# Prompt attention: a head's weighted sum over its last 512 queries issued as one piece of eight key blocks, behind the next head's second row block

## The chip, the cores and the metric

The kernel runs on one core of a Trainium2 chip. The metric is the device time of one execution in microseconds (us). Three runs of the kernel before gave 2279.73, 2285.48 and 2282.09 us, so the median is 2282.09 us.

## What is computed

The program is one inference step of a small decoder trunk with 1024 prompt tokens (and 32 sample tokens). After the first layer and the shared keys and values come 16 heads of causal attention of the prompt with itself, with a learned decay. Cut to what matters here:

```
s = einsum('bqhd,bkhd->bhqk', q, k) * (1.0 / sqrt(HEAD_DIM))      # HEAD_DIM = 64
decay = cq[..., :, None] - ck[..., None, :]                       # cumulative log forget sums
s = where(k_pos[None, :] <= q_pos[:, None], s + decay, -inf)
p = softmax(s, axis=-1)
o = einsum('bhqk,bkhd->bqhd', p, v)                               # the weighted sum
```

After it come the output projection and the second layer's MLP.

## The kernel before, in words

A head's 1024 queries are cut into 8 row blocks of 128. A row block has a running number `n` over all heads, 0 to 127; `n % 8` is its place `i` in the head, and it has `(i + 1) * 128` keys. Four engines pass a row block on, each in a loop over `n` that is written out in a fixed order:

- TensorE (PE), `prompt_pe`: `score(n + 3)` multiplies queries and keys for the row block three ahead (L1635, L1636, and the causal mask last, L1639). `turn(n)` transposes the probabilities of row block `n`, 128 keys at a time (L1650), into two PSUM banks that take turns, four transposes to a bank.
- VectorE (DVE), `prompt_dve`: in turn `n` it does `norm(n + 1)` (a reciprocal, L1744, and a scaling of the row block, L1747), sometimes `out` (two copies of a finished weighted sum out of PSUM, L1755), and `top(n + 3)` (the row maximum of the scores, L1739).
- ScalarE (ACT), `prompt_act`: in turn `n` it copies the transposes of row block `n` out of PSUM into `pT` (`turned(n)`, L1723) and then does the exponentials of row block `n + 3` (`exp(n + 3)`, L1712).
- GpSimd (POOL) splits the finished sums of two heads into a high and a low part (L1786 and L1788), once in two heads for each half of the queries.

The weighted sum of a head is done in two halves of 512 queries. `weigh(n, kb0, kb1)` adds the key blocks `kb0` to `kb1 - 1` of the half that row block `n` ends, with matmuls that fill 64 columns of the array each, two side by side (L1674 and L1678, behind the diagonal L1676 and L1680). The first half has four key blocks and stands at `n % 8 == 4`. The second half has eight. Before the change it stands in two pieces behind the next head's row blocks: key blocks 0 to 3 after `turn` of the next head's first row block (`n % 8 == 0`), key blocks 4 to 7 after `turn` of its third (`n % 8 == 2`). The piece with key block 0 waits until ACT has copied all transposes of the head (`t_ev`), and until the bank's last sum has been copied out (`o_ev`). DVE copies the second half out in its turn `n % 8 == 3`, and the first half of the head before in its turn `n % 8 == 1`.

Between these, in turns 14 to 17, PE does the last weighted sums of the sample tokens (`weigh_sample`, L1418, and `turn_sample`, L1440), which DVE copies out in `spread_sample` (L1557).

The loads of the next heads' queries, keys and values are issued by the SP queue, which waits for `q_full` and `o_full`.

Of the kernel before, what the change touches and what calls it, by code (L numbers as in the profile page):

```python
# [26 lines left out]
def decoder_step(nc, ins, outs):  # L27
# [18 lines left out]
    NQ = T // P  # L46
# [15 lines left out]
    with ExitStack() as ctx:  # L62
# [1368 lines left out]
        def weigh_sample(pe, u, bank):  # L1431
            pe.wait_ge(s_vg[u], 64)
            pe.wait_ge(p_ev, 2 * (u + 1))
            pe.wait_ge(s_in, 16)
            weigh_part(pe, u, bank, (0, 1, 2)).then_inc(s_pv, 1)

        def turn_sample(pe, u, bank):
            pe.wait_ge(s_osb, u + 1)
            for q in range(4):
                last = pe.transpose(ps[:, bank, q * P:(q + 1) * P], o_sb[:, q * P:(q + 1) * P], ident[:, :])  # L1440
            last.then_inc(s_otr, 1)
# [140 lines left out]
        def probs_of(i, c0, c1):  # L1582
            if P_AT[i] == 4:
                return p_hi2[:, c0:c1]
            return p_lo4[:, P_AT[i] * 512 + c0:P_AT[i] * 512 + c1]

        def quads_to(n):
            return 12 * (n // NQ) + sum(i // 4 + 1 for i in range(n % NQ))
# [29 lines left out]
        def prompt_pe(pe):  # L1618
            pe.wait_ge(one_rows, 2)

            def score(n):
                hh, i = divmod(n, NQ)
                e, w = hh % 2, (i + 1) * P
                if i == 0:
                    pe.wait_ge(stacked[e], STACK * (hh // 2 + 1))
                if n >= S_BACK[i]:
                    pe.wait_ge(q_exp, n - S_BACK[i] + 1)
                if n == 0:
                    pe.wait_ge(v_ev, 2 * NTT)
                if n == 3:  # L1630
                    pe.wait_ge(s_oc, 4 * 2)
                b = S_AT[i]
                for s in range(0, w, 512):
                    c = min(512, w - s)
                    pe.matmul(ps[:, b + s // 512, 0:c], q_a[e][:, i * P:w], k_a[e][:, s:s + c], start=True, stop=False)  # L1635
                    pe.matmul(ps[:, b + s // 512, 0:c], q_b[e][0:HD + 2, i * P:w], k_b[e][0:HD + 2, s:s + c],  # L1636
                              start=False, stop=(s + c < w))
                at_ = i * P % 512
                pe.matmul(ps[:, b + i * P // 512, at_:at_ + P], ident_b[:, :], causal_b[:, :], start=False,  # L1639
                          stop=True).then_inc(q_full, 1)  # L1640

            def turn(n):
                i = n % NQ
                pe.wait_ge(q_nrm, n + 1)
                for s in range(0, i + 1, 4):
                    nq = quads_to(n) + s // 4
                    if nq >= 2:
                        pe.wait_ge(t_ev, nq - 1)
                    for kb in range(s, min(s + 4, i + 1)):
                        last = pe.transpose(ps[:, 4 + nq % 2, (kb - s) * P:(kb - s + 1) * P],  # L1650
                                            probs_of(i, kb * P, (kb + 1) * P), ident[:, :])
                    last.then_inc(t_full, 1)

            def weigh(n, kb0, kb1):


                hh, g = n // NQ, n // 4 % 2
                av = 2 * hh + g
                if kb0 == 0:
                    pe.wait_ge(t_ev, quads_to(n + 1))  # L1660
                    pe.wait_ge(v_in[hh % 2], 16 * (hh // 2 + 1))
                    if av >= 2:
                        pe.wait_ge(o_ev, 2 * (av - 1))
                    if av == 0:
                        pe.wait_ge(s_oc, 4)
                    if av == 1:
                        pe.wait_ge(p_ev, 8)
                    if av == 4:
                        pe.wait_ge(s_oc, 4 * 4)
                for kb in range(kb0, kb1):  # L1670
                    x = pT[g][:, kb, :].rearrange("p (r c) -> p r c", c=P)
                    d, v, bank = kb - 4 * g, v_h[hh % 2][:, kb, :], 6 + av % 2
                    if d <= 0:
                        pe.matmul(ps[0:HD, bank, 0:2 * P], v, x[:, 0:4:3, :], start=(kb == 0), stop=False)  # L1674
                    else:
                        outer = pe.matmul(ps[0:HD, bank, P:2 * P], v, x[:, 3, :], start=False, stop=(d == 3))  # L1676
                    if d <= 1:
                        pe.matmul(ps[HD:P, bank, 0:2 * P], v, x[:, 1:3, :], start=(kb == 0), stop=False)  # L1678
                    elif d == 2:
                        pe.matmul(ps[HD:P, bank, P:2 * P], v, x[:, 2, :], start=False, stop=True).then_inc(o_full, 1)  # L1680
                    else:
                        outer.then_inc(o_full, 1)

            for n in range(3):
                score(n)
            for n in range(NBLK):
                if n + 3 < NBLK:
                    score(n + 3)
                turn(n)
                if n % NQ == 4:  # L1690
                    weigh(n - 1, 0, 4)
                elif n % NQ in (0, 2) and n >= NQ:
                    weigh(n - n % NQ - 1, 2 * (n % NQ), 2 * (n % NQ) + 4)
                if n == 14:
                    pe.wait_ge(o_ev, 6)
                    weigh_sample(pe, 2, O_BANK[2])
                if n == 15:
                    turn_sample(pe, 2, O_BANK[2])
                if n == 16:
                    pe.wait_ge(s_oc, 4 * 3)  # L1700
                    weigh_sample(pe, 3, O_BANK[3])
                if n == 17:
                    turn_sample(pe, 3, O_BANK[3])
            weigh(NBLK - 1, 0, NQ)
# [442 lines left out]
        @block.tensor  # L2147
        def _(pe):

            front_pe(pe)  # L2150
            mlps[0].pe(pe)
            heads_pe(pe)
            sample_pe_end(pe)
            pe.wait_ge(const_ready, 13)
            prompt_pe(pe)
            proj_o.pe(pe)
            mlps[1].pe(pe)
# [64 lines left out]
```

## Time and profile before

| | |
|---|---|
| median of three runs | 2282.09 us |
| the profiled execution, its own time | 2281.51 us |
| its span, first to last instruction | 2278.5 us |
| PE busy | 2236.0 us (98%) |
| DVE, ACT, POOL busy | 1036.8, 575.6, 612.8 us |
| stretch of the prompt attention | 1176 to 1436 us |
| in it PE, DVE, ACT busy | 242.05, 205.92, 182.12 us |
| one head in the steady part | 15.1 us (two heads 30.15) |

A PE busy of 98% is made by the MLPs ahead of the attention and behind it. In the attention the engines wait for one another in turn, so that stretch is read from its own rows: who waits for whom, and what stands in time order around the place that the change moves. "Idle before" in brackets is how long the engine did nothing before that row and what ended it.

### The profile page before, as it was taken

The page shows a single profiled execution, that of the slowest core. Times are in us where ns is not written, and L with a number is a line of the kernel's source. Part 1 is how long each engine was busy: PE and PEld are TensorE (multiplying, and loading weights), DVE is VectorE, ACT ScalarE, POOL GpSimd, SP SyncE. Part 2 cuts the span into 40 slices and gives each one's busy share as a digit, 9 for nine tenths or more (in the row PEclk, how much of TensorE's full clock was granted, in tenths as well). Part 3 has the DMA queues.
Part 4 walks back from the last instruction along what each step waited for, and adds up shares of the span by engine and source line. Part 5 has one row for each costly group of instructions (what it writes and reads, how often), then busy time and mean ns, then how long its engine had stood idle before and what let it go on. Part 6 is the DMA issues. An engine that isn't in the chain of part 4 may idle for free.

```text
span 2278.5 us, 36833 instructions
## 1 busy us (share of the span) xinstructions
PE 2236.0 (98%) x14447; PEld 2077.3 (91%) x14447; DVE 1036.8 (46%) x1760; ACT 575.6 (25%) x1264; POOL 612.8 (27%) x445
## 2 busy tenths in 40 slices
PE   8999999999999999999999999999999999999999
PEld 8999999999999977777776777999999999999999
DVE  7842332433333676543146888335333433324332
ACT  5420110110101333333145777322110100101101
POOL 6233333333333522100001112353333333322240
PEclk9999999999999999999999999999999999999999
DMA  5111111111111114445565654011111111111112
GB/s 154 41 47 47 47 47 47 46 47 43 43 47 47 66 65 150 153 130 165 179 171 119 144 117 107 28 47 47 47 47 44 45 43 47 47 47 47 47 56 77
DMA packets 195852, 170.01 MB, mean 75 GB/s; under 512 B 28880, under 2 KB 169472, under 8 KB 195687
## 3 DMA queue, kind: packets, MB, share of 16 engines
q1 hardware_dynamic: 155493, 141.50, 21.8%
q10 hardware_dynamic: 40202, 26.23, 3.7%
q8 instruction: 122, 2.00, 0.4%
q14 instruction: 35, 0.29, 0.0%
HBM read 137.55 MB, written 30.50 MB: 74 GB/s over the span
## 4 chain that ended last, share of the span: by engine, by line
PE 86%; DVE 7%; ACT 3%; DMA 2%; issue 1%; POOL 0%; SPq 0%; ACTq 0%; DVEq 0%
PE ps L368 35%; PE ps L633 29%; PE ps L881 12%; DVE stat L1739 2%; PE ps L495 2%; ACT pT L1723 1%; PE ps L1674 1%; DMA k_b<-cum_dram 1%; DVE p_lo L1747 1%; PE ps L896 1%; PE ps L1922 1%; PE ps L1650 1%; PE ps L1376 1%; PE ps L1396 1%; DVE tmp_b L445 1%
## 5 line engine op out<-in xcount | busy, mean ns | idle before, releaser
L368 PE MATMUL ps<-xn_hi,w_lo 128*128 128x352 f32 x1528 | 494.9, 324 | 4.9 <-DVE h L711 4.2
L368 PE MATMUL ps<-xn_lo,w_hi 128*128 128x352 f32 x1528 | 489.8, 321 | 0.0
L368 PE MATMUL ps<-xn_hi,w_hi 128*128 128x352 f32 x1528 | 489.4, 320 | 0.0
L633 PE MATMUL ps<-hid_hi,w_lo 128*128 128x352 f32 x1440 | 464.5, 323 | 0.0
L633 PE MATMUL ps<-hid_lo,w_hi 128*128 128x352 f32 x1440 | 461.9, 321 | 0.0
L633 PE MATMUL ps<-hid_hi,w_hi 128*128 128x352 f32 x1440 | 461.4, 320 | 0.0
L335 POOL CAST w_hi<-w_raw 128x1024 fp32r<-128x1024 f32 x132 | 139.2, 1055 | 994.9 <-issue 506.2
L711 DVE TENSOR_TENSOR h<-ps,h 128x352 f32<-128x352 f32 x360 | 185.8, 522 | 413.1 <-PE ps L633 413.1
L672 ACT ACTIVATE tmp_b<-tmp_a 128x352 f32<-128x352 f32 x192 | 94.9, 498 | 1076.6 <-DVE tmp_a L694 1076.6
L337 POOL TENSOR_TENSOR w_lo<-w_raw,w_hi 128x1024 fp32r<-128x1024 f32 x132 | 319.1, 2417 | 10.6
L368 PEld LDWEIGHTS ps<-xn_hi,w_lo 128*128 128x128 f32 x1528 | 286.6, 188 | 7.9 <-DVE h L711 5.3
L368 PEld LDWEIGHTS ps<-xn_lo,w_hi 128*128 128x128 f32 x1528 | 287.1, 188 | 0.5
L368 PEld LDWEIGHTS ps<-xn_hi,w_hi 128*128 128x128 f32 x1528 | 286.4, 187 | 0.0
L633 PEld LDWEIGHTS ps<-hid_lo,w_hi 128*128 128x128 f32 x1440 | 270.5, 188 | 0.0
L633 PEld LDWEIGHTS ps<-hid_hi,w_lo 128*128 128x128 f32 x1440 | 270.2, 188 | 0.0
L633 PEld LDWEIGHTS ps<-hid_hi,w_hi 128*128 128x128 f32 x1440 | 269.9, 187 | 0.0
L694 DVE SCALAR_TENSOR_TENSOR tmp_a<-ps,rms 128x352 f32<-128x352 f32 x192 | 99.3, 520 | 372.7 <-PE ps L368 372.4
L698 DVE TENSOR_TENSOR hid_lo<-tmp_b,hid_hi 128x352 fp32r<-128x352 f32 x192 | 224.3, 1219 | 60.9 <-ACT hid_hi L675 60.9
L881 PE MATMUL ps<-kv_lo,xn_hi 128*128 128x512 f32 (+1 forms) x400 | 162.1, 405 | 1.5 <-issue 0.8
L881 PE MATMUL ps<-kv_hi,xn_hi 128*128 128x512 f32 (+1 forms) x400 | 157.5, 394 | 0.0
L881 PE MATMUL ps<-kv_hi,xn_lo 128*128 128x512 f32 (+1 forms) x400 | 157.2, 393 | 0.0
L1739 DVE TENSOR_REDUCE stat<-ps 128x1 f32<-128x128 f32 (+7 forms) x128 | 96.3, 752 | 35.5 <-PE ps L1639 35.0
(266 smaller groups left out, 2828.3 us busy)
## 6 DMA issues: line engine op xcount, KB each, us to landing
w_raw<-in_w_up SPq DMA_DIRECT2D x64, 512.0 KB, 4.0
w_raw<-in_w_down SPq DMA_DIRECT2D x60, 512.0 KB, 3.4
out<-tok_out ACTq DMA_DIRECT2D x32, 256.0 KB, 2.2
qk_dram<-turn_hi ACTq DMA_DIRECT2D x32, 256.0 KB, 2.4
qk_dram<-turn_lo ACTq DMA_DIRECT2D x32, 256.0 KB, 2.9
k_page<-in_cache_k SPq DMA_DIRECT2D x32, 256.0 KB, 3.4
v_page<-in_cache_v SPq DMA_DIRECT2D x16, 512.0 KB, 9.5
q_a<-qk_dram SPq DMA_DIRECT2D x32, 256.0 KB
```

Of the source, the lines that this page charges most:

```text
L335: pool.tensor_copy(hi[:, par, :], w_raw[:, par, :]).then_inc(w_split, 1)
L337: pool.tensor_tensor(lo[:, par, :], w_raw[:, par, :], hi[:, par, :].bitcast(F32), ALU.subtract).then_inc(w_split, 1)
L368: last = pe.matmul(ps[:, bank, 0:CH], w, x(k, c), start=(k == 0 and i == 0), stop=(k == nk - 1 and i == 2))
L445: eng.tensor_tensor(tmp_b[:, c, :], tmp_b[:, c, :], self.slots[self.sum_at(m, c) % len(self.slots)], ALU.add).then_inc(self.acc, 1)
L495: last = pe.matmul(ps[:, n % 2, 0:CH], w, x, start=(k == 0 and i == 0), stop=(k == GT - 1 and i == 2))
L633: last = pe.matmul(ps[:, NC * (dm % 2) + c, 0:CH], w, x, start=(k == 0 and i == 0), stop=(k == GT - 1 and i == 2))
L672: act.activation(tmp_b[:, c, :], tmp_a[:, c, :], ACT.Square).then_inc(self.sq, 1)
L694: dve.scalar_tensor_tensor(tmp_a[:, c, :], ps[:, NC * (j % 2) + c, 0:CH], 0.0, rms[:, c], ALU.max, ALU.mult).then_inc(self.relu, 1)
L698: dve.tensor_tensor(hid_lo[:, self.uhalf * GT + j, chunk(c)], tmp_b[:, c, :], hid_hi[:, self.uhalf * GT + j, chunk(c)].bitcast(F32), ALU.s ...
L711: dve.tensor_tensor(h[:, dm, chunk(c)], ps[:, NC * (dm % 2) + c, 0:CH], h[:, dm, chunk(c)], ALU.add).then_inc(self.added, 1)
L881: last = pe.matmul(ps[0:w, g % 4, :], x, y, start=(k == 0 and j == 0), stop=(k == KT - 1 and j == 2))
L1739: dve.tensor_reduce(stat[:, 0, n % 4:n % 4 + 1], scores_of(i), AX, ALU.max, negate=True).then_inc(q_max, 1)
```

## The change

In PE's loop, the second half's weighted sum is no longer issued in two pieces of four key blocks at `n % 8 == 0` and `n % 8 == 2`. It is issued in one piece of eight at `n % 8 == 1`, behind the scores of the next head's fifth row block (640 keys) and the transposes of its second. Nothing else is edited; no instruction is added or taken away, and the rows of DVE, ACT, POOL and SP keep their order.

```
                 turn(n)
                 if n % NQ == 4:
                     weigh(n - 1, 0, 4)
-                elif n % NQ in (0, 2) and n >= NQ:
-                    weigh(n - n % NQ - 1, 2 * (n % NQ), 2 * (n % NQ) + 4)
+                elif n % NQ == 1 and n >= NQ:
+                    weigh(n - 2, 0, NQ)
                 if n == 14:
```

The order on PE, at a head's end in the middle of the loop, between the transpose of the next head's first row block and its second. `k_a` and `q_a` are keys and queries, `p_lo` the probabilities, `pT` their transposes, `v_h` the values. Before, the last two matmuls of the first piece and what follows them:

```order
L1674 MATMUL ps<-pT_154,v_h_158 64x256
L1678 MATMUL ps<-pT_154,v_h_158 64x256
L1635 MATMUL ps<-k_a_148,q_a_144 128x512
L1636 MATMUL ps<-k_b_150,q_b_146 128x512
L1635 MATMUL ps<-k_a_148,q_a_144 128x128
L1636 MATMUL ps<-k_b_150,q_b_146 128x128
L1639 MATMUL ps<-causal_b,ident_b 128x128
L1650 MATMUL ps<-ident,p_lo_151 128x128 x2
```

After the change, from the transpose of the first row block on:

```order
L1650 MATMUL ps<-ident,p_lo_151 128x128
L1635 MATMUL ps<-k_a_148,q_a_144 128x512
L1636 MATMUL ps<-k_b_150,q_b_146 128x512
L1635 MATMUL ps<-k_a_148,q_a_144 128x128
L1636 MATMUL ps<-k_b_150,q_b_146 128x128
L1639 MATMUL ps<-causal_b,ident_b 128x128
L1650 MATMUL ps<-ident,p_lo_151 128x128 x2
L1674 MATMUL ps<-pT_154,v_h_158 64x256
```

The scores over 640 keys no longer have a piece of the weighted sum ahead of them.

The order on PE at the next step, ahead of the scores over 768 keys (sixth row block). Before, they come straight behind the two transposes:

```order
L1650 MATMUL ps<-ident,p_lo_151 128x128 x2
L1635 MATMUL ps<-k_a_148,q_a_144 128x512
L1636 MATMUL ps<-k_b_150,q_b_146 128x512
L1635 MATMUL ps<-k_a_148,q_a_144 128x256
L1636 MATMUL ps<-k_b_150,q_b_146 128x256
L1639 MATMUL ps<-causal_b,ident_b 128x128
```

After the change, the end of the piece of eight and what follows it:

```order
L1676 MATMUL ps<-pT_154,v_h_158 64x128
L1678 MATMUL ps<-pT_154,v_h_158 64x256
L1676 MATMUL ps<-pT_154,v_h_158 64x128
L1680 MATMUL ps<-pT_154,v_h_158 64x128
L1676 MATMUL ps<-pT_154,v_h_158 64x128
L1635 MATMUL ps<-k_a_148,q_a_144 128x512
L1636 MATMUL ps<-k_b_150,q_b_146 128x512
L1635 MATMUL ps<-k_a_148,q_a_144 128x256
L1636 MATMUL ps<-k_b_150,q_b_146 128x256
L1639 MATMUL ps<-causal_b,ident_b 128x128
```

All 15 matmuls of the second half now stand between those transposes and the 768-key scores.

The order on PE in turns 17 and 18, where the sample's last transposes (`o_sb`) stand. Before:

```order
L1650 MATMUL ps<-ident,p_lo_151 128x128 x2
L1440 MATMUL ps<-ident,o_sb 128x128 x4
L1635 MATMUL ps<-k_a_147,q_a_143 128x512
L1636 MATMUL ps<-k_b_149,q_b_145 128x512
L1635 MATMUL ps<-k_a_147,q_a_143 128x256
```

After the change:

```order
L1676 MATMUL ps<-pT_154,v_h_159 64x128
L1680 MATMUL ps<-pT_154,v_h_159 64x128
L1676 MATMUL ps<-pT_154,v_h_159 64x128
L1440 MATMUL ps<-ident,o_sb 128x128 x4
L1635 MATMUL ps<-k_a_147,q_a_143 128x512
```

The sample's transposes too now have the whole piece ahead of them.

## Rows read from the trace of the kernel before

**Rows 1.** Busy time by stretch: the attention, then two heads of it.

```profile
core 0: us, PE busy (x) PEld busy (x) DVE busy (x) ACT busy (x) POOL busy (x), PEclk, DMA share, GB/s
...
1176.00:1436.00 260.00, 242.05 (x1993) 180.89 (x1994) 205.92 (x456) 182.12 (x450) 37.38 (x36) 0.98 0.56 131
...
1316.72:1346.88 30.16, 28.58 (x227) 21.54 (x226) 25.33 (x56) 22.38 (x56) 3.77 (x4) 1.00 0.55 123
```

**Rows 2.** Waits of DVE in twelve steady heads (total us, times, longest).

```profile
DVE stat L1739 <- PE ps L1639: 18.5, 36, 0.8
```

**Rows 3.** Chain of waits through a head's end (start us, us, what).

```profile
1324.70 0.60 ACT pT L1723
...
1328.25 0.82 DVE stat L1739
```

**Rows 4.** PE in time order, same head's end (start us, us, engine, line, operation).

```profile
1324.98 0.28 PE L1650 MATMUL ps<-ident,p_lo 128*128 128x128 f32 x1
1325.35 0.43 PE L1674 MATMUL ps<-pT,v_h 128*64 128x256 f32 x1
...
1326.91 0.38 PE L1674 MATMUL ps<-pT,v_h 128*64 128x256 f32 x1
...
1327.22 0.50 PE L1635 MATMUL ps<-k_a,q_a 128*128 128x512 f32 x1
...
1327.98 0.23 PE L1639 MATMUL ps<-causal_b,ident_b 128*128 128x128 bf16 x1
1328.05 0.39 PE L1650 MATMUL ps<-ident,p_lo 128*128 128x128 f32 x2
...
1328.99 0.23 PE L1639 MATMUL ps<-causal_b,ident_b 128*128 128x128 bf16 x1
...
1329.48 0.43 PE L1674 MATMUL ps<-pT,v_h 128*64 128x256 f32 x1
...
1330.72 0.50 PE L1635 MATMUL ps<-k_a,q_a 128*128 128x512 f32 x1
```

**Rows 5.** DVE in time order, same head's end.

```profile
1326.54 0.87 DVE L1755 COPY oT<-ps 64x256 f32<-64x256 f32 x2
1328.25 0.82 DVE L1739 TENSOR_REDUCE stat<-ps 128x1 f32<-128x640 f32 x1 [0.84 <-PE ps L1639]
...
1329.59 0.95 DVE L1739 TENSOR_REDUCE stat<-ps 128x1 f32<-128x768 f32 x1
```

**Rows 6.** PE, the head's end before that one.

```profile
1309.87 0.43 PE L1674 MATMUL ps<-pT,v_h 128*64 128x256 f32 x1
```

**Rows 7.** DVE, the head's end before that one.

```profile
1311.06 0.88 DVE L1755 COPY oT<-ps 64x256 f32<-64x256 f32 x2
...
1314.18 0.94 DVE L1739 TENSOR_REDUCE stat<-ps 128x1 f32<-128x768 f32 x1
```

**Rows 8.** POOL, the head's end before that one.

```profile
1312.69 1.28 POOL L1788 TENSOR_TENSOR o_lo<-oT,o_hi 128x512 fp32r<-128x512 f32 x1
```

**Rows 9.** PE's weight loads at the edges of the two pieces.

```profile
1318.34 0.13 PEld L1674 LDWEIGHTS ps<-pT,v_h 128*64 128x64 f32 x1 [0.17 <-issue]
...
1327.22 0.19 PEld L1635 LDWEIGHTS ps<-k_a,q_a 128*128 128x128 f32 x1 [0.39 <-issue]
```

**Rows 10.** PE at the sample's last transposes.

```profile
1221.63 0.60 PE L1440 MATMUL ps<-ident,o_sb 128*128 128x128 f32 x4
```

**Rows 11.** DVE at the copies behind them.

```profile
1222.35 0.60 DVE L1557 COPY o_s<-ps 64x32 f32<-64x32 f32 x4
```

**Rows 12.** PE where the third head's scores begin.

```profile
1203.58 0.48 PE L1635 MATMUL ps<-k_a,q_a 128*128 128x128 f32 x1 [2.59 <-DMA k_b<-cum_dram]
```

**Rows 13.** PE, three places with a longer wait or behind one.

```profile
1322.14 0.95 PE L1650 MATMUL ps<-ident,p_lo 128*128 128x128 f32 x7 [1.08 <-ACT pT L1723]
...
1413.45 0.98 PE L1650 MATMUL ps<-ident,p_lo 128*128 128x128 f32 x7 [1.93 <-DVE p_lo L1747]
...
1414.90 1.97 PE L1650 MATMUL ps<-ident,p_hi 128*128 128x128 f32 x8
```

**Rows 14.** Busy time and granted clock (PEclk) behind the longest of those waits.

```profile
1414.00:1416.00 2.00, 1.96 (x13) 1.67 (x11) 1.96 (x4) 1.64 (x6) 1.92 (x2) 0.71 0.78 234
```

## Prediction, made before the changed kernel was run

> **What bounds the kernel now.** I read the page first: PE is busy 98% of the span, but that is the MLPs. The busy time by stretch [rows 1] singles out the attention: in its 260.0 us PE is busy 242.05, DVE 205.92, ACT 182.12, so no engine fills it. Two steady heads take 30.16 us, of which PE works 28.58 and DVE 25.33. The waits [rows 2] say who is late: in twelve heads DVE's row maximum waits 36 times, 18.5 us in all, for PE's causal mask, the last matmul of a score block. The chain of waits [rows 3] shows when: ACT copies the last transposes out until 1325.30, PE then starts the first piece of the weighted sum, and DVE's next row on the chain is the 640-key maximum at 1328.25. From there the chain stays on DVE until the exponentials of the head's last row block, then passes to ACT and PE, and so to the next head's end. So one head costs what this ring costs, and the place the change moves lies on it.
>
> **The parts, for one head's end.** Nothing is added or removed: 15 weighted-sum matmuls move on PE. What counts is when DVE gets the 640-key and the 768-key scores.
>
> What goes. The first piece no longer stands ahead of the 640-key scores. DVE had finished the copies at 1326.54 + 0.87 = 1327.41 and waited 0.84 us for them [rows 5]. They now start behind the transpose of 1324.98 [rows 4] and are there well before 1327.41. So the 640-key maximum starts 0.84 us earlier, and the scaling of the fourth row block behind it too.
>
> What is late next. The 768-key maximum followed 1.34 us after the 640-key one (1328.25 to 1329.59 [rows 5]) without a wait. DVE would be ready for it at 1327.41 + 1.34 = 1328.75. But its scores now stand behind the whole piece. I add up PE from the transpose at 1324.98, with durations of [rows 4]:
>
> - To the mask of the 640-key scores. The same stretch one block larger, 1328.05 to 1328.99, takes 0.94; one transpose less (0.11, half the step of 0.22 between 256-column matmuls) and 128 columns less in two single-pass matmuls (0.11 together) leave 0.72. I take 0.77, an estimate between that and the 0.83 that it would be if the columns saved nothing.
> - Mask, and two transposes until the weighted sum starts: with three it is 1328.99 to 1329.48, 0.49; less 0.11 is 0.38.
> - The piece of eight. The pieces take 1325.35 to 1327.22 = 1.87 and 1329.48 to 1330.72 = 1.24, together 3.11. One end and one start go: the eighth row of the first piece starts at 1326.91, a step of 0.22 later is 1327.13, so the end costs 0.09, and a start about 0.06. 2.96 remains.
> - The 768-key scores to their mask: 640 keys took 1327.22 to 1327.98, 0.76; 128 columns more in one matmul that shows, 0.06: 0.82.
> - Mask to DVE (1327.98 to 1328.25): 0.27.
>
> The sum is 0.77 + 0.38 + 2.96 + 0.82 + 0.27 = 5.20 us, so the 768-key maximum starts at 1330.18 and not at 1329.59: 0.59 us later. The wait of 0.84 us goes, and one of 1330.18 - 1328.75 = 1.43 comes.
>
> At the head's end before, POOL splits sums at the same time, and the places differ a little. Its first piece starts at 1309.87 [rows 6], so its transpose at 1309.50 by the same distance of 0.37, and the 768-key maximum would start at 1314.70 instead of 1314.18 [rows 7]: 0.52 us later.
>
> What lies beside it. The waits of the piece are met already: the last copy of `pT` ends at 1325.30 [rows 3], and the piece would start at about 1326.1. The 640-key exponentials come earlier, the second row block's copy to `pT` too. Behind the 768-key scores PE has 1.24 us less to do before the 896-key scores, so those come earlier than before, not later. ACT's copies wait for transposes that come about 0.9 us later than before (behind the mask of 1328.99, now at about 1329.91), ahead of the 768-key exponentials, which wait for the late maximum anyway. So from the 768-key maximum on everything on the ring shifts by the same 0.5 to 0.6 us; I find nothing with slack on it. DVE's copy of the sum is no closer to a wait, and the loads of heads are issued behind `o_full` and `q_full` that come within 1 us of before, against landings that no steady head waits for.
>
> **Which head's ends count.** The second half is moved at 15 places. The first (`n` = 9) has no price: the third head's scores wait 2.59 us for a load [rows 12], which was issued before. Of the places from the fourth head on, seven are like [rows 4] and six like [rows 6]: 7 x 0.59 + 6 x 0.52 = 7.3 us. At the third head (`n` = 17) the sample's transposes stand behind the piece. They started at 1221.63 [rows 10]; the first piece is gone from ahead of them (1.87, of which some 0.1 becomes a wait for the sample's copies), the whole is added (2.96 and 0.1): 1222.8. They take 0.60, so the copies, before at 1222.35 [rows 11], start at 1223.45, and the 768-key maximum stands behind them on DVE: 1.1 us. In all 8.4 us.
>
> The profiled execution took 2281.51 us itself, 0.6 under the median of the runs. 2281.5 + 8.4 = 2289.9; on the median, 2282.1 + 8.4 = 2290.5 us. I predict 2290.5, slower by 0.37%. What this measurement can tell from no change is about 0.3%, 6.8 us.
>
> Bounds of one term: had the pieces no seam at all to give back and the 640-key stretch its 0.83, the shift would be 0.80 and 0.73, in all 11.3 us (2293.4). The other end is the first rival.
>
> The Trainium skill bears on the seam: "TensorEngine Tiling (Array Packing)", section Key Properties, says that changing the tiling mode drains TensorE. The 64-column matmuls and the 128-column ones are two modes, and one piece has two changes fewer for each head. By that rule the merging alone is a gain, and the more so the more a drain costs; the 0.15 us I take per head is what the starts of matmuls show of it.
>
> **Rivals.**
>
> 1. The seam costs more than the matmul starts show. The weight loads sit idle 0.17 us ahead of a piece and 0.39 behind the first one [rows 9]. If both go, 0.56 us and not 0.15, and the 640-key stretch takes 0.72, the shift is 0.59 - 0.41 - 0.05 = 0.13 (and 0.06), in all 7 x 0.13 + 6 x 0.06 + 0.6 = 1.9 us: 2284 us, no change that can be told. For it speaks the idle itself; against it that most of that is the array finishing the last rows, which the steps between starts include already.
>
> 2. Faster: the wait taken away is the only one that counts. It is decided at the 768-key maximum: if its scores are there by 1328.75, nothing new is late, and the ring keeps the 0.84 us. At the seven plain heads' ends that is 5.9 us. At the six with POOL it is nothing: the 512-wide scaling would then start at 1311.94 + 0.74 + 0.19 = 1312.87 (copies' end [rows 7], maximum and reciprocal), inside POOL's subtraction of 1312.69 to 1313.97 [rows 8], and the 768-key maximum behind it could hardly start before the 1314.18 of now. Less 1 us lost at the sample: 2277 us. Against it: the piece of eight would have to take 1.5 us and not 2.96, and its steps of 0.22 us are those of 256 columns in two passes.
>
> The Trainium skill, "SBUF — State Buffer", section Who interferes with whom, has the port pair of VectorE and GpSimd as an exclusive lock that the later one waits out whole. By that rule, too, this rival has nothing to win at the POOL head's ends.
>
> 3. Slower by more: PE's clock falls. In the ring's POOL heads PE waits 1.08 us ahead of the seven transposes [rows 13], and the granted clock over two such heads is 1.00 [rows 1], the level of 2.4 GHz. The new order makes this wait longer. Behind the 768-key scores PE has the 1.24 us of the second piece less to do, and those scores, once ready 0.37 us ahead of their maximum (1328.99 + 0.23 against 1329.59 [rows 4, 5]), are then just in time: PE runs up to 0.87 us further ahead of the ring, and the wait grows to at most 1.95. PE must also wait for the 768-key exponentials before the 1024-key scores, which takes part of it, so I take the middle, 1.5 us (an estimate). Once, behind a wait of 1.93 us, the clock fell to 0.71 in the mean of two microseconds [rows 14], and eight transposes took 1.97 us [rows 13], where seven at full clock take 0.95, so eight 1.06. With the scores behind them that is about 1.3 us a time. Six times it adds 8 us: 2298 us.
>
> That the change does not do what it says I rule out but for the first rival: the order on PE is fixed.
>
> **How the numbers follow.** The forecast 0.70, the first rival 0.14, the second 0.06, the third 0.10. The forecast's own range is 2287 to 2294 (3 us down for a seam between mine and the first rival's, 3 up for its upper bound and the runs' scatter). Of its 0.70, 0.10 falls under 0.3%. So slower by over 0.3%: 0.60 + 0.10 = 0.70; within: 0.14 + 0.10 = 0.24; faster: 0.06. The range that holds 8 in 10 takes in part of the first and third: 2284.5 to 2296.5.
>
> **What would show it.** In the changed kernel the 640-key maximum starts straight behind the copies, with no wait, and the 768-key one waits about 1.4 us for PE's mask. From the single transpose to it are 5.2 us. Two heads take 31.25 us and not 30.16. The wait ahead of the seven transposes in POOL heads is about 1.5 us at clock 1.00. The total of DVE's waits for PE rises from 18.5 to about 26 us in the twelve heads. It would be wrong if the piece of eight took under 2.6 us, if the period of two heads stayed under 30.6, or if the stretches outside 1176 to 1436 us changed.

## The result, and the profile after

The changed kernel took 2292.14 us in the median of four runs (2289.62 to 2296.26), the kernel before 2281.34 us beside it. The ratio is 1.0046, with a 95% interval of 1.0034 to 1.0058: by the ratio 10.5 us slower, between 7.8 and 13.2 (the two medians differ by 10.8). All gains and losses below are worked out from the ratio in this way. Forecast were 8.4 us and 2290.5 us. The profiled execution took 2289.62 us, its span 2287.6 us, 9.1 more than before.

The steady part answers to [rows 1]; the columns are the same:

```profile
1227.31:1258.62 31.31, 28.31 (x225) 21.68 (x225) 26.22 (x56) 22.18 (x56) 5.16 (x6) 1.00 0.57 130
...
1289.98:1321.34 31.36, 28.35 (x225) 21.71 (x225) 26.22 (x57) 22.19 (x56) 3.77 (x4) 1.00 0.53 119
...
1227.31:1415.34 188.03, 170.00 (x1345) 130.09 (x1345) 157.34 (x337) 133.13 (x336) 24.01 (x26) 1.00 0.55 125
```

Two heads take 31.36 us and not 30.16, at the same granted clock of 1.00, and PE is busy no longer in them (28.35 against 28.58 us). All of the loss is waiting. The last row is twelve heads; the same stretch of the kernel before, between the same two 896-key maxima, is

```profile
1226.26:1407.17 180.91, 171.16 (x1345) 129.03 (x1344) 151.99 (x336) 134.23 (x336) 24.02 (x26) 1.00 0.58 129
```

so 7.12 us of the 9.1 are made there, 0.59 us a head. DVE's busy time rises by 5.35 us in it although it does the same work: 4.8 of that is a scaling that is held by POOL at six of the twelve ends and takes 1.35 us where it took 0.55 (below).

PE at a head's end without POOL work (a plain end), in time order, answers to [rows 4]:

```profile
1329.59 0.28 PE L1650 MATMUL ps<-ident,p_lo 128*128 128x128 f32 x1
...
1330.39 0.23 PE L1639 MATMUL ps<-causal_b,ident_b 128*128 128x128 bf16 x1
...
1330.78 0.43 PE L1674 MATMUL ps<-pT,v_h 128*64 128x256 f32 x1
...
1333.73 0.51 PE L1635 MATMUL ps<-k_a,q_a 128*128 128x512 f32 x1
...
1334.56 0.23 PE L1639 MATMUL ps<-causal_b,ident_b 128*128 128x128 bf16 x1
```

and DVE at the same end to [rows 5]:

```profile
1331.16 0.87 DVE L1755 COPY oT<-ps 64x256 f32<-64x256 f32 x2
1331.96 0.81 DVE L1739 TENSOR_REDUCE stat<-ps 128x1 f32<-128x640 f32 x1
...
1332.87 0.49 DVE L1747 TENSOR_SCALAR p_lo<-p_lo,stat 128x512 f32<-128x512 f32 x1
1334.83 0.96 DVE L1739 TENSOR_REDUCE stat<-ps 128x1 f32<-128x768 f32 x1 [1.47 <-PE ps L1639]
```

The 640-key maximum now follows the copies without a wait, and the 768-key one waits 1.47 us for PE. From the single transpose to it are 1334.83 - 1329.59 = 5.24 us; before, 1329.59 - 1324.98 = 4.61. The difference of 0.63 is the head's loss.

At the end before it POOL splits finished sums (a POOL end). DVE there answers to [rows 7], POOL to [rows 8]:

```profile
1315.11 0.88 DVE L1755 COPY oT<-ps 64x256 f32<-64x256 f32 x2
...
1316.95 1.35 DVE L1747 TENSOR_SCALAR p_lo<-p_lo,stat 128x512 f32<-128x512 f32 x1
1318.78 0.96 DVE L1739 TENSOR_REDUCE stat<-ps 128x1 f32<-128x768 f32 x1 [0.49 <-PE ps L1639]
```

```profile
1316.74 1.27 POOL L1788 TENSOR_TENSOR o_lo<-oT,o_hi 128x512 fp32r<-128x512 f32 x1
```

The 512-wide scaling, moved up by the wait that went, now starts 0.2 us into POOL's subtraction and takes 1.35 us, where it takes 0.49 alone. At the same end of the kernel before it started late in that subtraction (1312.69 to 1313.97 [rows 8]) and hardly lost by it:

```profile
1313.70 0.55 DVE L1747 TENSOR_SCALAR p_lo<-p_lo,stat 128x512 f32<-128x512 f32 x1
```

In both it ends about 0.28 us after the subtraction: 1314.25 against 1313.97, and 1318.30 against 1318.01. The long scaling costs nothing here, for PE's scores come 0.49 us later still.

The waits of twelve heads answer to [rows 2] (total us, times, longest), DVE's and PE's:

```profile
DVE stat L1739 <- PE ps L1639: 20.0, 36, 1.5
```

```profile
PE ps L1650 <- ACT pT L1723: 12.8, 12, 1.4
PE ps L1635 <- ACT p_lo L1712: 5.9, 13, 1.0
```

The second of PE's rows is new: the 1024-key scores wait for the 768-key exponentials. The chain of waits now goes from PE's eight transposes through the whole piece to DVE:

```profile
1328.16 1.06 PE ps L1650 x8
...
1333.81 0.43 PE ps L1635
...
1334.83 0.96 DVE stat L1739
```

### The profile page after: what moved, and what is told of

Same layout as the page of the kernel before. It is cut to its first block, busy times and chain, and to the rows that moved or that the text cites. A ratio compares the mean times of both kernels' runs of the same rounds, so it can differ in the third digit from the quotient of the medians.

```text
span 2287.6 us, 36833 instructions
## 1 busy us (share of the span) xinstructions
PE 2238.9 (98%) x14447; PEld 2082.7 (91%) x14447; DVE 1041.4 (46%) x1760; ACT 573.7 (25%) x1264; POOL 613.7 (27%) x445
## 4 chain that ended last, share of the span: by engine, by line
PE 89%; DVE 7%; issue 1%; ACT 1%; DMA 1%; ACTq 0%; SPq 0%; DVEq 0%
PE ps L368 35%; PE ps L633 29%; PE ps L881 12%; DVE stat L1739 2%; PE ps L495 2%; PE ps L1650 2%; PE ps L1674 2%; PE ps L1635 1%; PE ps L1636 1%; PE ps L896 1%; DVE p_lo L1747 1%; PE ps L1922 1%; PE ps L1954 1%; PE ps L1376 1%; PE ps L1396 1%
```

## The experiments

The diffs are against the kernel before; where only added lines of `weigh` are shown, the two removed lines are those of whole0. Each is compared with the kernel before on the same chip. The first four stood in one comparison, the three with POOL in another, and the changed kernel itself was timed in neither.

**whole0: the place of the piece, one way.**

```
-                elif n % NQ in (0, 2) and n >= NQ:
-                    weigh(n - n % NQ - 1, 2 * (n % NQ), 2 * (n % NQ) + 4)
+                elif n % NQ == 0 and n >= NQ:
+                    weigh(n - 1, 0, NQ)
```

> The piece of eight key blocks stands at the first row block (n % 8 == 0), ahead of the 640-key scores, and nothing else changes. Theory (what stands ahead of the score block that DVE waits for sets the head): the second piece of 1.24 us, less 0.15 of merging, joins the first ahead of the 640-key scores, so their maximum starts 1.09 us later, and nothing behind it has slack. 13 head's ends of 1.05 and one of 1.1 us at the sample: about +15 us, two steady heads 32.3 us. Rival (one piece instead of two gains by saved mode changes wherever it stands): 0.56 us saved per head and more than half of the rest hidden, +0 to +5 us.

2295.03 us; the ratio is 1.0059 (1.0045 to 1.0073), so 13.5 us slower, 10.3 to 16.7. Two steady heads, between the 896-key maxima at 1321.49 and 1353.75, take 32.26 us. DVE at a head's end:

```profile
1331.30 0.87 DVE L1755 COPY oT<-ps 64x256 f32<-64x256 f32 x2
1334.10 0.82 DVE L1739 TENSOR_REDUCE stat<-ps 128x1 f32<-128x640 f32 x1 [1.92 <-PE ps L1639]
```

The wait of 0.84 [rows 5] has become 1.92, by the 1.09 us that stand ahead of these scores in addition. The merging gains no more than was counted; the place sets the time. The rival, with 0 to 5 us, is out.

**whole2: the other way.**

```
+                elif n % NQ == 2 and n >= NQ:
+                    weigh(n - 3, 0, NQ)
```

> The piece of eight key blocks stands at the third row block (n % 8 == 2), behind the 768-key scores. Theory: the 640-key maximum starts straight behind DVE's copies (0.84 us earlier), the 768-key one 1.34 behind it without a wait, and the 896-key one waits for PE about 0.2 us (scores ready 6.43 us after the single transpose), which leaves 0.62 us gained at a head's end without POOL work. Where POOL splits, its subtraction holds the 512-wide scaling back until about 2.3 us after the copies, as in the changed kernel (1.35 us instead of 0.49), and nothing is gained. 7 x 0.62 and 0.5 at the sample: -4.9 us, 0.2%. Two steady heads 29.5 us. Rival (eight blocks in one piece are too long for PE wherever they stand): +5 to +10 us like the changed kernel.

2284.53 us; the ratio is 1.0012 (1.0003 to 1.0021), 2.7 us slower (0.7 to 4.8) where 4.9 faster was expected. Two heads take 30.42 us (1317.77 to 1348.19), not 29.5. PE and DVE at a plain head's end show what the expectation left out:

```profile
1326.01 0.28 PE L1650 MATMUL ps<-ident,p_lo 128*128 128x128 f32 x1
...
1327.76 0.50 PE L1635 MATMUL ps<-k_a,q_a 128*128 128x512 f32 x1 [0.53 <-ACT p_lo L1712]
```

```profile
1332.19 0.87 DVE L1755 COPY oT<-ps 64x256 f32<-64x256 f32 x2 [0.92 <-PE ps L1680]
1333.23 1.09 DVE L1739 TENSOR_REDUCE stat<-ps 128x1 f32<-128x896 f32 x1 [0.17 <-PE ps L1639]
```

PE runs so far ahead that the 768-key scores wait 0.53 us for the exponentials of the fourth row block, whose PSUM banks they take. The piece behind them ends that much later, and DVE's copies of its own sum, which stand ahead of the 896-key maximum, wait 0.92 us for it. So the forecast's rule (find who is late next) held, and I had not followed it past the first engine. Neither wait stands there in the changed kernel, where the piece of 2.95 us lies ahead of the 768-key scores. The rival, with 5 to 10 us wherever the piece stands, is out too.

**four12: two pieces of four, one place later each.**

```
+                elif n % NQ in (1, 2) and n >= NQ:
+                    weigh(n - n % NQ - 1, 4 * (n % NQ - 1), 4 * (n % NQ))
```

> Two pieces again, key blocks 0 to 3 at n % 8 == 1 (behind the 640-key scores) and 4 to 7 at n % 8 == 2 (behind the 768-key scores). Theory: the single transpose to the 768-key maximum takes 5.24 - 2.95 + 1.87 = 4.16 us instead of 5.24, so that maximum is 0.45 us earlier than in the kernel before, and the 896-key one 0.25 earlier, at the plain head's ends; at the POOL ones nothing, since the held scaling sets the time. About -2 us, two steady heads 29.9 us. Rival (it is the single place behind row block two that costs, not the length of the piece there): as slow as the changed kernel.

2281.44 us; the ratio is 1.0001 (0.9993 to 1.001), and two heads take 29.98 us (1315.21 to 1345.19) against 30.16. The trace has 0.18 us for two heads of the theory's 0.26; the time of the whole can't tell its 2 us from nothing. What it does tell is the rival: with the same matmuls begun at the same place, behind the second row block, but only four key blocks of them, the 10.5 us of the changed kernel are gone. It is the length ahead of the 768-key scores that costs.

**late_only: the change without its first two places.**

```
+                elif n % NQ in (0, 2) and NQ <= n < 3 * NQ:
+                    weigh(n - n % NQ - 1, 2 * (n % NQ), 2 * (n % NQ) + 4)
+                elif n % NQ == 1 and n >= 3 * NQ:
+                    weigh(n - 2, 0, NQ)
```

> The changed order from the fourth head's start on (n >= 24), the order before for the two head's ends ahead of it. Theory: the 13 steady ends cost 0.59 each by the trace of the changed kernel, 7.7 us; the ends at n = 9 and n = 17 cost 0 and 1.1. So +7.7 us against the kernel before, and 1 us less than the changed kernel. Rival (the early part, with loads in flight and a clock that falls there, makes a good part of the loss): +4 to +6 us.

2291.14 us; the ratio is 1.0044 (1.0027 to 1.006), 10.0 us slower, 6.2 to 13.7. Expected were 7.7 us. The steady ends carry the loss: two heads take 31.32 us (896-key maxima at 1306.72 and 1338.04). The rival's 4 to 6 us lie just below the interval. The 1 us of the third head is not told apart: this interval and that of the changed kernel overlap far more widely than that.

**pool_late: POOL's work put elsewhere, PE's order as before.**

```
                 pool.wait_ge(o_ev, 8 * r + 6 + 2 * g)
+                if 0 < r < 6:
+                    pool.wait_ge(q_nrm, NQ * (2 * r + 2 + g) + (3 if g else 5))
```

> PE's order of the kernel before; only POOL's splitting of finished sums is put off for head pairs 1 to 5: the first half's until the next head's fifth row block is scaled (its work then lies beside DVE's copies and the 896-key maximum), the second half's until the third row block of the head after it is scaled (beside the copies and the 640-key maximum). Theory (POOL's subtraction holds DVE's scaling, on the ring): the 768-wide scaling falls from 1.22 to 0.62 us and the 512-wide from 0.55 to 0.49, so 5 x 0.65 = 3.2 us less in all, two steady heads 29.5 instead of 30.16. Rival (DVE's copies are held by POOL just as the scalings are): the stall moves to the copies, no change.

2277.4 us; the ratio is 0.9982 (0.9973 to 0.9991), 4.1 us faster, 2.1 to 6.2, where 3.2 was expected and the rival had nothing. Two heads take 29.49 us (1317.30 to 1346.79). The scaling in question as it was in the kernel before, then DVE and POOL at the same place of pool_late:

```profile
1317.92 1.22 DVE L1747 TENSOR_SCALAR p_lo<-p_lo,stat 128x768 f32<-128x768 f32 x1
```

```profile
1316.39 0.88 DVE L1755 COPY oT<-ps 64x256 f32<-64x256 f32 x2
1317.30 1.09 DVE L1739 TENSOR_REDUCE stat<-ps 128x1 f32<-128x896 f32 x1
...
1318.50 0.62 DVE L1747 TENSOR_SCALAR p_lo<-p_lo,stat 128x768 f32<-128x768 f32 x1
```

```profile
1316.50 0.61 POOL L1786 CAST o_hi<-oT 128x512 fp32r<-128x512 f32 x1 [17.40 <-DVE p_hi L1747]
1317.19 1.27 POOL L1788 TENSOR_TENSOR o_lo<-oT,o_hi 128x512 fp32r<-128x512 f32 x1
```

POOL now ends at 1318.46, just ahead of the scaling, which takes 0.62 us and not 1.22 as before. The copies, now beside POOL's cast (L1786), and the maximum, now beside its subtraction, keep their 0.88 and 1.09 us. So the subtraction holds a scaling from SBUF to SBUF and not a maximum that reads PSUM, and the cast does not hold copies out of PSUM; a copy well inside the subtraction, or a scaling beside the cast, stands in none of these rows. The Trainium skill ("SBUF — State Buffer", section Who interferes with whom) describes an exclusive lock that whoever comes second waits out whole, and says that not every VectorE instruction takes part in it. The trace agrees: the held scalings end a fixed time after the subtraction however early they began, the 512-wide one 0.28 to 0.29 us (above), the 768-wide one 0.42 us, in the kernel before (1319.14 against 1318.72) as in the changed one (1323.76 against 1323.34).

**after_pool: the same on the changed kernel.**

> The changed kernel with POOL's splitting put off as in pool_late. Theory: the 512-wide scaling falls from 1.35 to 0.49 us, which gives nothing since the 768-key maximum waits for PE anyway (its wait grows from 0.49 to about 1.4), and the 768-wide one from 1.22 to 0.62, which is on the ring: 5 x 0.6 = 3.0 us less than the changed kernel, so +6 us against the kernel before, two steady heads 30.75. Rival (the held 512-wide scaling is part of the changed kernel's loss): 5 x 1.4 = 7 us less, about +2 us.

The edit is the one of pool_late on top of the change. 2288.48 us; the ratio to the kernel before is 1.003 (1.002 to 1.004), 6.8 us slower, 4.6 to 9.1, where 6 was expected and the rival had 2. Two heads take 30.73 us (1319.96 to 1350.69). At the end where the 512-wide scaling was held, the wait behind it has grown, as the theory has it:

```profile
1315.59 0.49 DVE L1747 TENSOR_SCALAR p_lo<-p_lo,stat 128x512 f32<-128x512 f32 x1
1317.40 0.96 DVE L1739 TENSOR_REDUCE stat<-ps 128x1 f32<-128x768 f32 x1 [1.32 <-PE ps L1639]
```

The scaling takes 0.49 us instead of 1.35, and the wait behind it is 1.32 instead of 0.49. The held scaling was no part of the loss. At the next end, where POOL's second subtraction now lies beside the 640-key maximum (it ends at 1331.24), it holds the scaling a little, again to 0.28 us after its own end, and PE is later still:

```profile
1330.88 0.64 DVE L1747 TENSOR_SCALAR p_lo<-p_lo,stat 128x512 f32<-128x512 f32 x1
...
1332.84 0.96 DVE L1739 TENSOR_REDUCE stat<-ps 128x1 f32<-128x768 f32 x1 [1.32 <-PE ps L1639]
```

Against pool_late, with POOL out of the way in both, the change costs 30.73 - 29.49 = 1.24 us for two heads: 0.62 for each, the plain head's 0.63.

**four12_pool: four12 and pool_late together.**

> Key blocks 0 to 3 at n % 8 == 1 and 4 to 7 at n % 8 == 2, with POOL's splitting put off as in pool_late. Theory: both held scalings were on the ring here (512-wide 1.36, 768-wide 1.22), so both go: 0.54 and 0.60 per pair of heads, two steady heads 28.85 instead of 29.98, in all 5 x 1.1 = 5.7 us less than four12 and about 7 us less than the kernel before (0.3%). Rival (with the holds gone PE is late): the 768-key and 896-key maxima wait and only half of it comes, -4 us.

The edits are those of four12 and pool_late. 2275.13 us; the ratio is 0.9973 (0.9964 to 0.9982), 6.2 us faster than the kernel before, 4.1 to 8.2: the lowest median of all, where about 7 was expected and the rival had 4. Two heads take 29.01 us (1312.28 to 1341.29), 0.97 less than four12, where the theory had 1.13 and the rival half of that. Most of the 0.16 that is missing lies at the POOL end:

```profile
1309.61 0.96 DVE L1739 TENSOR_REDUCE stat<-ps 128x1 f32<-128x768 f32 x1 [0.24 <-PE ps L1639]
...
1311.26 0.88 DVE L1755 COPY oT<-ps 64x256 f32<-64x256 f32 x2
1312.28 1.09 DVE L1739 TENSOR_REDUCE stat<-ps 128x1 f32<-128x896 f32 x1
```

From the copies to the 768-key maximum it gained 0.56 us, as expected, although the maximum now waits for PE. But the 896-key maximum starts 0.14 us behind the end of the second copies, 0.27 behind PE's mask of 1312.01: it waits for PE too. In four12 it followed 0.02 us behind the copies. So PE is late by then, as the rival has it, but takes 0.13 us of the gain and not half.

Against pool_late the trace has 0.48 us less for two heads. Both stood in one comparison, at 2275.13 and 2277.4 us, but their intervals against the kernel before overlap, and a direct comparison of the two was not made.

## Why the prediction was right

**Where the ring is.** Right. The loss is all in the attention's waits, and whole0 and four12 moved it both ways by what stands ahead of the scores that DVE waits for.

**The sum for one head.** 5.20 us forecast from the single transpose to the 768-key maximum, 5.24 measured. The piece of eight took 1330.78 to 1333.73, 2.95 us for the 2.96 of the two pieces less 0.15. The new wait was 1.47 for 1.43. The shift was a little low, 0.63 measured for 0.59, nearly all of it in the stretch to the mask of the 640-key scores (0.80 for the estimated 0.77). At the POOL ends it was 0.57 for 0.52, since two heads make 1.20 together.

**The number of places.** The thirteen steady ends: 0.59 each over twelve, and between the last 896-key maximum of the twelve and the output projection, 28.65 us before (1407.17 to 1435.82) and 29.23 after (1415.34 to 1444.57), another 0.58. Together 7.7 us, forecast 7.3.

**The first two places.** Forecast 0 and 1.1 us. In the changed kernel, the sample's last two sets of copies, of which the second stands ahead of the 768-key maximum on DVE:

```profile
1214.23 0.61 DVE L1557 COPY o_s<-ps 64x32 f32<-64x32 f32 x4 [0.76 <-PE ps L1440]
...
1223.40 0.61 DVE L1557 COPY o_s<-ps 64x32 f32<-64x32 f32 x4 [2.95 <-PE ps L1440]
```

From the first copies to the second are 9.17 us. In the kernel before, where the second stood at 1222.35 [rows 11], they were 7.90:

```profile
1214.45 0.61 DVE L1557 COPY o_s<-ps 64x32 f32<-64x32 f32 x4 [0.76 <-PE ps L1440]
```

So the place cost 1.27 us, about as forecast. Beside it lie 1.8 us more ahead of the attention, where nothing was changed (PE's first score of the attention starts at 1177.70 and not 1175.91), and about 2 us less behind the load that the third head waits for. The prediction counted a change outside the attention as a sign of being wrong. It is scatter between executions: with the same instructions ahead of it, that first score starts between 1175.63 (whole0) and 1179.03 (whole2). In the kernel before, PE waited 2.59 us for that load [rows 12] and the clock fell behind it; in the changed kernel it waited 0.37 us and the clock stayed:

```profile
1205.38 0.33 PE L1635 MATMUL ps<-k_a,q_a 128*128 128x128 f32 x1 [0.37 <-DMA k_b<-cum_dram]
```

That is not the change's: in the changed kernel's profile the clock had been low, 0.53 in the mean, from 1176 to 1186 us, before any instruction that was moved, and PE reached the load later for that. In late_only, with the first place as before, it waited 2.60 us again, and in whole0, where the first place too has the whole piece, 2.08. So how the 9.1 us of the profiles are put together differs from run to run in its early part, and the 10.5 us of the runs stay 1.5 us above the 9.0 (7.7 + 1.27) that the mechanism accounts for, within their interval. What makes up that rest is open, and so is whether it is there at all.

**The wrong check.** The total of DVE's waits for PE was to rise to about 26 us and rose to 20.0. I had put 1.4 us on all twelve ends. At six of them POOL held the scaling, which took 0.9 us of the wait: 6 x 1.47 + 6 x 0.49, and the 0.7 of the other two maxima at each of the twelve, are 20.2. The hold stood in the text, but as the price of the second rival only.

**"From the 768-key maximum on I find nothing with slack."** It held for the shift. But PE does get ahead, and a wait of 0.4 us for the 768-key exponentials, which the third rival names, is new. It is free here, for the 1024-key maximum behind it does not wait for PE; the same kind of wait was what made whole2 slower.

**The rivals.** First: the seam gave 0.16 us and not 0.56 (3.11 against 2.95), so the idle time of the weight loads [rows 9] overstates it by more than three times. The Trainium skill ("TensorEngine Tiling (Array Packing)", section Key Properties) says that a change of the tiling mode drains TensorE; no row shows a drain by itself, but what the two changes saved here cost is within the 0.16 us. Second: it needed the 768-key scores 1.4 us sooner, and they came when the sum said; it is out. Third: the wait ahead of the seven transposes came out at 1.40 us for the 1.5 I took, and the clock stayed:

```profile
1326.76 0.95 PE L1650 MATMUL ps<-ident,p_lo 128*128 128x128 f32 x7 [1.40 <-ACT pT L1723]
...
1328.16 1.06 PE L1650 MATMUL ps<-ident,p_hi 128*128 128x128 f32 x8
```

Eight transposes take 1.06 us, full speed, and the granted clock over the twelve heads is 1.00.

## What to carry to other kernels

Moving work from ahead of one consumer's input can put it ahead of the next one's: add up, from one common instruction, when each of the next inputs comes and when its reader is free, and take the latest. A piece of work that fits one gap in two halves can cost more in one, even though merging saves its seams; what the seams save is read from the starts of the matmuls, not from the idle time of their weight loads. When an engine is moved ahead, follow it to its next wait and to the wait behind that, as whole2 shows.

## What the runs showed of the hardware

POOL's subtraction of 128 x 512 held a scaling that started 0.2 us into it for 1.35 us instead of 0.49, and the held 512-wide scalings read above ended 0.28 to 0.29 us after the subtraction. A maximum out of PSUM beside the same subtraction, and copies out of PSUM beside POOL's cast, kept their times (1.09 and 0.88 us). A move of POOL's work alone, with no instruction less, was worth 0.18% of the kernel. TensorE's clock stayed at 1.00 in the ring with a wait of 0.7 to 1.4 us in each head. Longer waits went both ways: behind one of 2.26 us in the changed kernel, at 1421.61, eight transposes took 1.92 us at a granted clock of 0.50, and the clock fell behind the load's 2.59 us before and 2.60 in late_only; behind 2.08 us in whole0, at 1203.45, seven transposes took the 0.96 us of full speed. Nor does it take a long wait: in the changed kernel the clock fell to 0.50 from about 1177 to 1186.5 us, behind eight microseconds in which PE was busy throughout and a wait of 0.42 us, while in the kernel before the same instructions with waits of 0.42 and 0.55 us kept it at 1.00. So the length of the last wait alone does not tell whether the clock falls.
